# GpSimd takes the residual add between output projection and feed-forward of a hybrid decoder layer

## The reference, cut to what matters

```python
mix = jnp.concatenate([lru_out, att_out], axis=-1) @ lw['w_out']
x = x + _rmsnorm(mix, lw['norm_post_mix'])        # the residual add that is moved
h = _rmsnorm(x, lw['norm_pre_ffn'])
f = (jax.nn.silu(h @ lw['ffn_w_gate']) * (h @ lw['ffn_w_up'])) @ lw['ffn_w_down']
x = x + _rmsnorm(f, lw['norm_post_ffn'])          # a second residual add, not moved
gate = jax.nn.sigmoid(x @ lw['ple_w_gate'])
x = x + _rmsnorm(gate * (p @ lw['ple_w_proj']), lw['ple_norm'])
```

## Time and profile before

| | |
|---|---|
| median of 3 runs | 3055.14 us (3049.95 to 3056.22) |
| the profiled execution: time | 3055.49 us |
| its span (first to last instruction) | 3053.7 us |
| PE busy | 2902.9 us, 95% |
| VectorE busy | 1801.4 us, 59% |
| ScalarE busy | 1356.9 us, 44% |
| GpSimd busy | 233.7 us, 8% |
| VectorE adds of L2352 | 32 of 1.225 us, 16 of them in the passages |
| passages of the four groups | about 684 to 711, 1260 to 1287, 1878 to 1905, 2501 to 2530 us |

### The profile page before, as it was taken

One profiled execution on the slowest core, in us unless ns is written; L12 is line 12 of the kernel. 1 busy time (PEld: TensorE's weight loads), 2 busy tenths in 40 slices (PEclk: granted clock), 3 DMA queues, 4 the chain that ended last, 5 costly groups with the idle time before them and its releaser, 6 DMA issues.

```text
span 3053.7 us, 38188 instructions
## 1 busy us (share of the span) xinstructions
PE 2902.9 (95%) x14242; PEld 2368.2 (78%) x14242; DVE 1801.4 (59%) x2874; ACT 1356.9 (44%) x2491; POOL 233.7 (8%) x314
## 2 busy tenths in 40 slices
PE   7999999779999999999999999999999999999997
PEld 6778787557788887788888788788888778787865
DVE  6867767567356666665566666555656564333454
ACT  5655544534244445544444455444434453222233
POOL 0201011200000100001001101011011000000000
PEclk9999999879999999999999999999999999999998
DMA  5546343756654444543544345535332353222221
GB/s 182 182 141 229 130 147 115 235 183 198 195 145 122 122 120 138 170 128 99 136 117 110 103 127 179 138 94 138 107 102 73 113 172 105 87 89 90 80 81 52
DMA packets 377576, 402.57 MB, mean 132 GB/s; under 512 B 25642, under 2 KB 277846, under 8 KB 377393
## 3 DMA queue, kind: packets, MB, share of 16 engines
q1 hardware_dynamic: 360624, 341.32, 37.7%
q0 software_dynamic: 16768, 58.81, 5.4%
HBM read 341.19 MB, written 58.91 MB: 131 GB/s over the span
## 4 chain that ended last, share of the span: by engine, by line
PE 60%; DVE 11%; ACT 5%; issue 2%; POOL 0%; DMA 0%; SPq 0%; ACTq 0%; DVEq 0%; POOLq 0%
PE c_bank L2656 48%; PE b_S L2951 3%; PE b_O L2977 2%; DVE c_w L2334 2%; PE b_WT L2963 1%; PE b_S L2665 1%; PE b_O L2665 1%; ACT c_junk L2103 1%; DVE c_rows L2345 1%; DVE b_m L2541 1%; DVE c_rows L2352 1%; ACT b_p L2260 1%; DVE b_p L2534 1%; PE b_O L2979 1%; DVE c_hT L2372 1%
## 5 line engine op out<-in xcount | busy, mean ns | idle before, releaser
L2656 PE MATMUL c_bank<-c_hT,c_w 128*128 128x512 f32 (+1 forms) x4416 | 1027.5, 386 | 15.3 <-DVE c_hT L2372 15.3
L2656 PEld LDWEIGHTS c_bank<-c_hT,c_w 128*128 128x128 f32 x4416 | 797.0, 190 | 171.3 <-issue 19.0
L2656 PE MATMUL c_bank<-c_w,c_fT 128*128 128x512 f32 x2112 | 510.6, 394 | 0.5 <-DVE c_rows L2394 0.5
L2334 DVE TENSOR_TENSOR c_w<-c_raw,c_w 128x1024 fp32r<-128x1024 f32 x334 | 405.7, 1222 | 153.9 <-ACT c_w L2082 152.3
L2082 ACT ACTIVATE c_w<-c_raw 128x1024 fp32r<-128x1024 f32 x334 | 352.1, 1058 | 256.9 <-PE c_bank L2656 219.0
L2656 PEld LDWEIGHTS c_bank<-c_w,c_fT 128*128 128x128 f32 x2112 | 391.7, 188 | 87.9 <-issue 4.4
L2260 ACT ACTIVATE b_p<-b_S,b_nm 128x512 f32<-128x512 f32 (+3 forms) x288 | 180.0, 630 | 586.4 <-DVE b_nm L2542 586.4
L907 PE MATMUL a_bank<-a_w,a_hT 128*128 128x512 f32 x1152 | 284.3, 401 | 0.0
L2656 PE MATMUL c_bank<-c_w,c_hT 128*128 128x512 f32 x1152 | 275.8, 395 | 7.7 <-DVE c_w L2334 4.0
L2656 PEld LDWEIGHTS c_bank<-c_w,c_hT 128*128 128x128 f32 x1152 | 217.5, 190 | 55.3 <-DVE c_w L2334 5.2
L907 PEld LDWEIGHTS a_bank<-a_w,a_hT 128*128 128x128 f32 x1152 | 213.5, 188 | 51.9 <-issue 3.8
(11 more groups left out here) (377 smaller groups left out, 3310.4 us busy)
## 6 DMA issues: line engine op xcount, KB each, us to landing
c_raw<-in_ffn_w_gate SPq DMA_DIRECT2D x88, 512.0 KB, 4.8
c_raw<-in_ffn_w_up SPq DMA_DIRECT2D x88, 512.0 KB, 4.2
c_raw<-in_ffn_w_down SPq DMA_DIRECT2D x88, 512.0 KB, 4.0
a_raw<-in_w_in SPq DMA_DIRECT2D x40, 1024.0 KB, 5.3
b_k<-split_kT SPq DMA_DIRECT2D x72, 256.0 KB, 4.9
b_v<-split_v SPq DMA_DIRECT2D x36, 512.0 KB, 3.6
c_raw<-in_w_out SPq DMA_DIRECT2D x32, 512.0 KB, 5.2
c_raw<-in_ple_w_gate SPq DMA_DIRECT2D x32, 512.0 KB, 4.2
```

The costliest lines, as they stand in the source:

```text
L2334: V.tensor_tensor(w[:, e[1] % SLOTS, 1], raw[:, n % RAW], w[:, e[1] % SLOTS, 0].bitcast(F32), ALU.subtract).then_inc(split_ready, 1)
L2656: ins = T.matmul(out, lhs(k, a), rhs(k, b), start=first and k == 0 and n == 0, stop=end and k == blocks - 1 and n == 2)
```

## The change

VectorE keeps the scaling; where it ran the add it now raises a new semaphore, `x1_scaled`. GpSimd waits for it and for the input rows, adds, and raises `x1_ready`. The fifth tile (the 8 sample rows) of the last group goes the same way. The residual add after the feed-forward (k = 2) stays on VectorE.

```diff
@@ gpsimd
+                if item[0] == "mix1t" and item[1] or item == ("near", 0):
+                    for t in turns(i, TILES, 0) if item == ("mix1t", 1) else (3,) if item[0] == "near" else (item[1] - 1,):
+                        pool.wait_ge(x1_scaled, nth(i, t))
+                        if t < TILES:
+                            pool.wait_ge(xr_in[t % 2], 16 * (4 * i + t // 2 + 1))
+                        else:
+                            pool.wait_ge(s_in, 48)
+                        nc.gpsimd.tensor_tensor(row(t), row(t), xr[:, t % 2] if t < TILES else s_xr[:], ALU.add).then_inc(x1_ready, 1)
                 if item == ("gate", 1):
                     for t in range(TILES):
                         pool.wait_ge(x1_ready, nth(i, t))
@@ vector
             def residual(i, k, t, src, dst, ready):
+                if k == 0:
+                    scaled(i, k, t, src, src).then_inc(x1_scaled, 1)
+                    return
                 link(scaled(i, k, t, src, src))
                 if t < TILES:
                     dve.wait_ge(xr_in[t % 2], 16 * (4 * i + k + t // 2 + 1))
                     V.tensor_tensor(dst, src, xr[:, t % 2], ALU.add).then_inc(ready, 1)
-                elif k == 0:
-                    dve.wait_ge(s_in, 48)
-                    V.tensor_tensor(dst, src, s_xr[:], ALU.add).then_inc(ready, 1)
                 else:
                     V.tensor_tensor(dst, src, s_row[:], ALU.add).then_inc(ready, 1)

             def normed(i, t):
+                dve.wait_ge(x1_ready, nth(i, t))
                 if t == TILES:
```

More of the change, by code:

```diff
@@ L1717, in feed @@
         std = [sem(f"c_std{n}") for n in range(4)]
+        x1_scaled = sem("c_x1_scaled")
         x1_ready = sem("c_x1_ready")
```

## The result

The changed kernel takes 3068.84 us (median of 5 runs, 3067.46 to 3070.91) beside 3055.11 for the kernel before on the same chip (5 runs): 1.0051 times as long, with an interval of 1.0039 to 1.0062. The forecast was 3070. The profiled executions differ by 15.0 us (3070.5 against 3055.5). From the scaling of tile 0 to the first gate operation of VectorE behind the passage, the four passages are 3.84, 3.03, 5.09 and 3.17 us longer, 15.1 in all. The stretches ahead of, between and behind them differ as well, by 0.6, -0.2, -0.7, -1.5 and 1.6 us, and these happen to cancel.

The account below looks back on a forecast made before the run. PE is busy 95%, but the passages are bound by a ScalarE-VectorE chain including the add. Three passages at 4.0 us plus 2.8 in the last give 14.8, 3070.3 on the profiled 3055.5; forecast 3070, range 3058 to 3080.

Parts of the forecast that it names:

- the links: ScalarE-VectorE chain in each passage: slower adds make tile 3 4.0 us late in three passages, 2.8 in the last.
- length of the add: GpSimd's two-input add of 1024 columns: 2.3 us, taken between 1.9 and 2.8, against 1.23 on VectorE.
- low halves of tiles 0 and 1 late by: Behind the scaling of tile 2: start 1.0 us late, delaying PE's first gate products 1.0, hidden behind the next link.
- last group, at its end: Fourth passage, where sample rows give the chain slack: 2.0 us late after tile 1, 2.5 after tile 2, 2.8 at the end.
- rival C: Add near 2.8 us gives 3076; second half-clock stretch on dense products, 1.7 a passage, 7 in all, 3077; both 3083; chance 0.16.
- who gets in first at tile 1: VectorE's `c_hn` scaling of tile 0 starts first and holds up GpSimd's add of tile 1, which ends 2.1 us late.
- the hop: From VectorE's scaled rows to GpSimd's start: 0.19 us, against 0.04 for VectorE's own add, so 0.15 more each time.
- rival A: No hold-up at tile 1: tiles 1, 2, 3 late by 1.2, 2.4, 3.0; 10.8 us in all, 3066; chance 0.17.
- The slack of 1.0 at tile 3: Tile 3's first-norm root lay ready 1.0 us while VectorE worked off `c_hn` of tile 2 and a weight chunk.
- the stores and loads that were put at nothing: `c_xr` loads issued 1.2 to 2.1 us later, and stores in a row after the last add, 4 x 0.5 us: no cost.
- Rival B: GpSimd adds in 1.1 us: unhindered, passages end 0.5 us early, 3053.5; hindered at tile 1 alone, 3058; chance 0.12.

Follow-up runs that it names:

- the run with GpSimd second: Changed kernel plus a small GpSimd memset before its add of tile 1, so VectorE's scaling is issued first: 3072.11 against 3053.29 us, 1.0065 times the kernel before.
- the one-input kernel: Changed kernel with GpSimd multiplying the row by one instead of adding the input rows: 3051.96 against 3053.29 us, 0.9999 times the kernel before.

## Why the prediction came out right

The total was right, 3070 for 3068.84. The way to it was not: one step was wrong and one term was left out of the sum. By the first, above all, the links came out 3.45 us too long in the sum; by the second 3.8 us are missing from it. That the two nearly cancel is luck.

| term, us | forecast | measured |
|---|---|---|
| GpSimd's start after VectorE's end | 0.19 | 0.08 |
| length of the add | 2.3 | 2.39 |
| add of tile 1 ends late by | 2.1 | 1.21 |
| low halves of tiles 0 and 1 late by | 1.0 | 0.02 |
| add of tile 2 ends late by | 3.4 | 2.45 |
| add of tile 3 ends late by | 4.0 | 3.01 |
| last group, at its end | 2.8 | 2.38 |
| four passages, up to tile 3 | 14.8 | 11.35 |
| half clock behind tile 3 | 0 (rival C: 7) | 3.8 |
| together | 14.8 | 15.1 |

- **Step that failed: who gets in first at tile 1.** The forecast let VectorE's scaling into `c_hn` start 0.11 after its predecessor and GpSimd 0.19 after it. GpSimd starts 0.08 after it (1270.50 against 1269.13 + 1.28 = 1270.41), and VectorE's next two-input scaling 0.23 after. The row taken for the hop, 0.19 behind a coefficient, was that of a VectorE operation of 6 columns and a GpSimd scaling, and did not hold for this pair; the 0.11 was a start without GpSimd. With starts 0.08 apart by its own figures, the forecast gave the order of them too much weight (0.55 against 0.17 for rival A). By the links alone rival A was right: 1.2, 2.4, 3.0 and 10.8 in all, against 1.21, 2.45, 3.01 and 11.35. The mechanism itself holds: whoever starts second waits for the other's whole instruction, as the run with GpSimd second shows (15.7 us up to tile 3).
- **Term left out: the clock.** Rival C had the half-clock stretch behind the longer wait, with 1.7 us each and 7 in all. It belonged in the sum: the wait before tile 3 was forecast at about 3 us, and the earlier trace rows showed what follows a wait of that size. It falls in three passages of four and costs 0.9, 2.1 and 0.8, 3.8 in all. Its size was off too: stretches like that of the earlier trace rows cost 0.9 and 0.8 us here, not 1.7, and the 2.1 are from one about twice as long.
- **Length of the add.** 2.3 was taken between the bounds of 1.9 and 2.8, and 2.39 measured. The choice rested on the second input not being free, which the one-input kernel bears out (1.05). The Trainium skill's figure ("GPSIMD Engine Reference", section "Elementwise — side-by-side cycle accounting") gave an estimate of 2.25, which is 6% short; the trace decides.
- **Low halves and PE's first products.** They were to come 1.0 late and come on time, since VectorE loses the add of 1.22 just where the scaling of tile 2 is 1.27 late. PE's wait for them was to grow by up to 1 us and fell from 3.51 to 3.00.
- **What was right step by step.** ScalarE's second norms wait for GpSimd (1.51, 1.65, 2.39); from the add of tile 1 to that of tile 3 it is 15.05 us between starts, forecast 15; PE's wait before the transposes of tile 3 is 2.76 (forecast about 3, before 0.97). The slack of 1.0 at tile 3 takes off 0.66 (2.45 to 1.79). The adds of tile 0 cost nothing. No cost of the stores and loads that were put at nothing is seen: the stretches outside of the passages differ by 1.6 us at most, in both directions, and cancel to 0.1. A cost of a few tenths there would not be seen.
- **Rival B** fell with the length of the add. That the start on another engine is free was its sound part: with an operation of 1.05 us the kernel is as fast as before, and its passages 0.8 to 1.6 us shorter, more than the 0.5 that B had.

## What to carry to other kernels

A link of a chain that one engine hands to a slower one costs the difference of the two lengths at each hand-over on the path, not the busy time that moved: here GpSimd took over 17 adds on an engine that is idle nine tenths of the time, and the kernel paid 1.2 us at each of tiles 1 and 3 and about 0.5 at tile 2. Price what the longer wait does to PE's clock in the same sum, and look for it on the products behind the wait, not in the wait. Where two engines hold each other up and start within 0.2 us of each other, work out both orders and treat them as even, unless a row shows the same pair of instructions.

## What the runs showed of the hardware

- A two-input scaling of VectorE and a two-input add of GpSimd don't share, they take turns by whole instruction. The one that starts 0.06 to 0.14 us later takes 3.33 to 3.48 us instead of 1.28 or 2.39. Nearly all of its work comes after the other's end: 1.08 of 1.28 us for VectorE (1273.97 against 1272.89), 2.26 of 2.39 for GpSimd (1272.24 against 1269.98). A lead of 0.06 us decided it either way. Behind GpSimd's one-input operation of 1.05 us, VectorE's scaling took 2.05 to 2.06.
- GpSimd's add of 1024 columns takes 2.39 us, its scaling of 1024 columns 1.05, while 512 columns take 0.69. The 8 sample rows cost it as much as 128 rows:

```profile
L2061 POOL TENSOR_TENSOR c_s_row<-c_s_row,c_s_xr x1: 2387/2387/2387, 2510.0 to 2510.0; 8x1024 f32<-8x1024 f32 x1
```

- VectorE's end to GpSimd's start took 0.08 us here, against 0.19 in the earlier trace rows.
- GpSimd's add isn't slowed by low halves that read a bank and one SBUF tile: beside them, from 1277.46, it takes 2.35.
- Waits of the changed kernel before tile 3 of 2.8 and 4.3 us were followed by full and by half clock (second and third passage). In the second the half-clock stretch lies earlier, on the first products of `near` (12 of them take 2.90 us from 1280.13), which also shortens the wait. What decides between the two, no run here tells. With 24, 8 and 32 spare transposes no half-clock stretch was left in the first three passages; in the fourth, which had none of them, one was left on the products ahead of tile 3.
